# GpSimd's constant loads wait for the low parts of two weight groups in place of the eighth weight piece

## The chip, the cores and the metric

The kernel runs on one core of one Trainium2 chip. The metric is the device time of one execution in microseconds (us), as the median of several runs. A profiled execution gives the rows of the trace; its times count from the start of its span, which is the stretch from its first to its last instruction.

## What is computed

The reference is a stack of transformer blocks over 256 tokens of width 1024, in float32: for each of two layers a gated feed-forward part, a mixer (latent attention in the first layer, attention with forget gates in the second), another feed-forward part and a gated embedding; then a second block with a multiscale pool, dilated attention, gates and a last norm. Only its first step matters here:

```python
h = h + FFN_HALF * swiglu(rms_norm(h, g_ffn1[i]), ffn1_w_in[i], ffn1_w_out[i])

def rms_norm(x, g):
    xf = x.astype(jnp.float32)
    y = xf * lax.rsqrt(jnp.mean(xf * xf, axis=-1, keepdims=True) + EPS)
    return (y * g.astype(jnp.float32)).astype(x.dtype)

def swiglu(x, w_in, w_out):
    gate, up = jnp.split(x @ w_in, 2, axis=-1)
    return (jax.nn.silu(gate) * up) @ w_out
```

The latent attention also needs positions, cosines and sines (`rope`), gains per head and a causal mask. These are the small constants of the change.

## The kernel before

**Weights in groups, each in two parts.** All weights stream from HBM through a ring of four slots. A weight group is 128 x 2048 float32 (1 MB). SyncE fetches it into `raw`; ScalarE rounds it to a high part `wh` (L1538); VectorE subtracts and gives the low part `wl` (L2086) and raises the semaphore `lo_done`; TensorE multiplies three products for each tile, `wh` by the high part of x, `wl` by the high part, `wh` by the low part (L628 to L630). A group of a feed-forward part's input gives 24 matmuls of 512 columns: 4 pieces of 128 rows, 2 tiles of tokens, 3 products. Before a group g TensorE waits for `lo_done` to be g - 1 (`wait_group`, L611), and before a chunk for its PSUM tile to have been read.

**The opening.** Groups 0, 1 and 2 of the first feed-forward part come in twelve pieces of 128 x 512, each with a DMA of its own. The first ten have semaphores of their own, `piece_in[0]` to `piece_in[9]`. ScalarE and VectorE split each piece (L1525, L2074). VectorE's pieces raise `piece_lo`, except for the twelfth, the last of group 2, which raises `lo_done` (DK is 8 here, and k counts from 0):

```python
dve.tensor_tensor(wl[:, k // 4, w], raw[:, k // 4, w], wh[:, k // 4, w].bitcast(F32), ALU.subtract)\
   .then_inc(piece_lo if k < DK + 3 else lo_done, 1)
```

So `lo_done` is 1 when group 2 is done, and 2 when group 3 is.

**The order of the work.** Each engine follows a program written out by hand, in order, and waits on semaphores. Chunk c of the first feed-forward part uses groups 2c and 2c + 1. For chunk 0 ScalarE splits groups up to 3 and then takes the silu of the two token tiles into `sg` (L1633), scaled by `rstd` (it waits for `rstd_done`, in `scaled`), and only then splits group 4. VectorE splits group 3, then multiplies into `a_n` (L2238), waiting for each silu, then splits groups 4 and 5, takes the second pair of `a_n`, and then runs `angles_reduced`, which waits for all eight small loads (`small_in`, L2151) and reads `posi` and `freq` (L2154 on); then groups 6 and 7.

**GpSimd.** Its program is: a memset, the wait of the change (L2942), eight issues of small loads (`tri`, `causal_f`, twice `hraw`, `rgain`, `bf`, `freq`, `posi`; L2943 to L2951), and then `norm(0)`: for each token tile it waits for the sum of squares `ssq` from ScalarE (L1570) and computes `rstd` in two instructions (`inverse_rms`, L2931 and L2932), of which the second raises `rstd_done`.

**SyncE's room.** A fetch of a group g from 6 on waits for `lo_done` to be g - 5 (`room`, L452), so that the slot's old content has been split.

Of the kernel before, what the change touches and what calls it, by code (L numbers as in the profile page):

```python
# [30 lines left out]
DK = D // P  # L31
# [122 lines left out]
def build(nc, I, out):  # L154
    with ExitStack() as ctx:
        def sem(name):
            return ctx.enter_context(nc.semaphore(name))
# [175 lines left out]
        piece_in = [sem(f"piece_in{i}") for i in range(DK + 2)]  # L333
# [4 lines left out]
        lo_done = sem("lo_done")  # L338
# [264 lines left out]
        def _(pe):  # L603
# [201 lines left out]
            def ffn(name, nname, r, after, r_after):  # L805

                g0, q0, _, _ = PLAN[name]

                def chunk(c, i=0):
# [302 lines left out]

            def ple(name, nname, r, after, r_after):
                g, q, _, _ = PLAN[name]
                ready = x_wait(nname)

# [391 lines left out]
        def _(act):  # L1508
# [321 lines left out]
            def ple(name, nname, r, after, r_after):  # L1830

                g, q, _, _ = PLAN[name]

                def sigmoids(t):
                    for n in range(2):
                        tile_ready(act, q + n, t, g + 3)
                        act.activation(gate[:, t, 512 * n:512 * n + 512], acc(q + n, t), ACT.Sigmoid,
                                       scale=scaled(r, t)).then_inc(acc_read[(q + n) % 2], 1)

                norm(nname, r, lambda t: split_to(g + 4), True)  # L1840
                for t in range(NT):
                    squares(r, t)
                sigmoids(0)
                split_to(g + 7)
                sigmoids(1)
                if after != "n8":
                    norm(after, r_after)
                    return

                for n, (t, k) in enumerate(BY_FEATURES):  # L1850
                    round_x(after, r_after, t, k)

                    if n in (8, 9):
                        squares(r_after, n - 8)
# [1065 lines left out]
        def _(pool):  # L2920
            steps = [0]

            def link(ins):

                steps[0] += 1
                ins.then_inc(p_step, 1)
                pool.wait_ge(p_step, steps[0])
# [11 lines left out]
                    link(pool.tensor_scalar(epsn[:, :], ssq[:, :], EPS / D, EPS * EPS, ALU.mult, ALU.add))  # L2939

            link(pool.memset(mhalf[:, :], -0.5))
            pool.wait_ge(piece_in[DK - 1], 16)  # L2942
            pool.dma_start(tri[:, :], I["c_mats"][1]).then_inc(small_in, 16)  # L2943
            pool.dma_start(causal_f[:, :], I["c_mats"][2]).then_inc(small_in, 16)
            for n in range(2):
# [197 lines left out]
```

## Time and profile before

| | us |
|---|---|
| median of 3 runs | 1302.85 |
| lowest, highest | 1302.75, 1304.57 |
| profiled execution, its time | 1302.51 |
| its span | 1300.7 |
| TensorE busy in the span | 1283.2 (99%) |
| VectorE, ScalarE, GpSimd busy | 929.7, 679.3, 125.9 |

The mean granted TensorE clock of the profiled execution is 0.999. A row of a timeline reads: start in us, duration in us, engine, line, operation, output and inputs, count, and in brackets how long the engine had been idle and what released it. Durations overlap a little at their ends, since engines are pipelined; the distance of two starts is the better measure for TensorE. Such a count as x9 merges equal instructions.

### The profile page before, as it was taken

The numbers are of one execution on the slowest core, as the hardware profiler recorded it, in microseconds if no ns is written. First come the engines' busy times: TensorE is split into PE (matmuls) and PEld (weight loads), VectorE is DVE, ScalarE is ACT, GpSimd is POOL, SyncE is SP. The second block draws the span as 40 slices with busy tenths as digits, with TensorE's granted clock in tenths as the row PEclk, the third lists the DMA queues.
The fourth block names the chain that finished last, engine by engine and source line by source line (L and its number), as shares of the span: only waits on it lengthen the run. The fifth ranks groups of instructions, "written<-read, shape, count | busy, mean of one in ns | idle before, by whom it ended". The sixth has DMA issues, their size and how long they took to land.

```text
span 1300.7 us, 16758 instructions
## 1 busy us (share of the span) xinstructions
PE 1283.2 (99%) x6242; PEld 1057.4 (81%) x6242; DVE 929.7 (71%) x1298; ACT 679.3 (52%) x976; POOL 125.9 (10%) x190
## 2 busy tenths in 40 slices
PE   9999999999999999999999999999999999999997
PEld 6888888888888888888887777888888887788886
DVE  6878948986678956677875677667895656655674
ACT  7444537755444546544445567644444735566542
POOL 1000003711000000000001230000000133200000
PEclk9999999999999999999999999999999999999999
DMA  9665645228565655666564643466564496445541
GB/s 311 216 201 189 210 140 203 66 82 263 191 194 194 202 186 162 195 194 194 194 196 158 231 162 119 149 194 194 194 226 154 170 293 215 156 137 179 174 149 33
DMA packets 149505, 236.29 MB, mean 182 GB/s; under 512 B 10080, under 2 KB 104464, under 8 KB 148928
## 3 DMA queue, kind: packets, MB, share of 16 engines
q1 hardware_dynamic: 144432, 222.26, 52.6%
q0 software_dynamic: 4640, 12.81, 3.3%
q8 instruction: 39, 0.64, 0.2%
q10 hardware_dynamic: 368, 0.37, 0.1%
q14 instruction: 26, 0.21, 0.0%
HBM read 233.27 MB, written 4.47 MB: 183 GB/s over the span
## 4 chain that ended last, share of the span: by engine, by line
PE 91%; DVE 4%; ACT 3%; issue 1%; POOL 0%; DMA 0%; POOLq 0%; SPq 0%; ACTq 0%; DVEq 0%
PE acc L628 20%; PE acc L630 20%; PE acc L629 20%; PE acc L661 7%; PE acc L662 7%; PE acc L665 7%; PE misc L704 4%; DVE wl L2086 1%; ACT wh L1538 1%; PE misc L1339 1%; PE misc L888 1%; PE misc L1195 1%; ACT xh L1584 0%; PE acc L868 0%; ACT hn L1570 0%
## 5 line engine op out<-in xcount | busy, mean ns | idle before, releaser
L2086 DVE TENSOR_TENSOR wl<-raw,wh 128x2048 fp32r<-128x2048 f32 x199 | 450.6, 2270 | 183.5 <-ACT wh L1538 182.8
L1538 ACT ACTIVATE wh<-raw 128x2048 fp32r<-128x2048 f32 x205 | 383.5, 1894 | 125.3 <-PE acc L665 104.2
L628 PE MATMUL acc<-wh,xh 128*128 128x512 f32 (+1 forms) x832 | 324.5, 390 | 3.3 <-DVE xl L2132 1.6
L630 PE MATMUL acc<-wh,xl 128*128 128x512 f32 (+1 forms) x832 | 322.5, 388 | 0.0
L629 PE MATMUL acc<-wl,xh 128*128 128x512 f32 (+1 forms) x832 | 322.3, 387 | 0.0
L628 PEld LDWEIGHTS acc<-wh,xh 128*128 128x128 f32 x832 | 156.2, 188 | 36.7 <-DVE wl L2074 1.8
L630 PEld LDWEIGHTS acc<-wh,xl 128*128 128x128 f32 x832 | 156.2, 188 | 32.2
L629 PEld LDWEIGHTS acc<-wl,xh 128*128 128x128 f32 x832 | 156.2, 188 | 31.1
L1633 ACT ACTIVATE sg<-acc,rstd 128x256 f32<-128x256 f32 x88 | 41.4, 475 | 240.4 <-PE acc L630 240.3
L2252 DVE STREAM_TRANSPOSE aT<-a_n 32x384 f32<-32x384 f32 (+1 forms) x256 | 137.1, 536 | 3.9
L661 PE MATMUL acc<-wh,ah 128*128 128x512 f32 x320 | 124.8, 390 | 0.0
L662 PE MATMUL acc<-wl,ah 128*128 128x512 f32 x320 | 124.5, 389 | 0.0
L628 PE MATMUL acc<-wh,zh 128*128 128x512 f32 x272 | 108.6, 399 | 0.5 <-DVE zl L2132 0.5
L630 PE MATMUL acc<-wh,zl 128*128 128x512 f32 x272 | 106.2, 390 | 0.0
L629 PE MATMUL acc<-wl,zh 128*128 128x512 f32 x272 | 106.0, 390 | 0.0
L665 PE MATMUL acc<-wh,al 128*128 128x512 f32 x320 | 98.5, 389 | 0.0
L2931 POOL TENSOR_SCALAR rstd<-ssq 128x1 f32<-128x1 f32 x19 | 9.4, 493 | 886.3 <-ACT hn L1570 886.2
L2238 DVE SCALAR_TENSOR_TENSOR a_n<-acc,rstd,sg 128x256 f32<-128x256 f32 x88 | 42.0, 483 | 48.1 <-ACT sg L1633 48.1
L1584 ACT ACTIVATE xh<-misc,gains 128x128 fp32r<-128x128 f32 x128 | 40.2, 365 | 68.4 <-PE misc L704 60.2
L665 PEld LDWEIGHTS acc<-wh,al 128*128 128x128 f32 x320 | 60.1, 188 | 12.5
L662 PEld LDWEIGHTS acc<-wl,ah 128*128 128x128 f32 x320 | 60.1, 188 | 12.4
L661 PEld LDWEIGHTS acc<-wh,ah 128*128 128x128 f32 x320 | 60.1, 188 | 12.3
(365 smaller groups left out, 1613.1 us busy)
## 6 DMA issues: line engine op xcount, KB each, us to landing
raw<-in_ffn_w_in_dram SPq DMA_DIRECT2D x170, 512.0 KB, 4.8
raw<-in_ffn_w_out_dram SPq DMA_DIRECT2D x88, 512.0 KB, 4.3
raw<-in_w_in_dram SPq DMA_DIRECT2D x64, 512.0 KB, 4.7
raw<-in_fox_w_in_dram SPq DMA_DIRECT2D x24, 512.0 KB, 4.2
raw<-in_ple_w_gate_dram SPq DMA_DIRECT2D x16, 512.0 KB, 4.4
raw<-in_mla_w_o_dram SPq DMA_DIRECT2D x8, 512.0 KB, 4.0
raw<-in_fox_w_o_dram SPq DMA_DIRECT2D x8, 512.0 KB, 4.4
raw<-in_w_out_dram SPq DMA_DIRECT2D x8, 512.0 KB, 4.4
```

Of the source, the lines that this page charges most:

```text
L628: pe.matmul(dst, hi, rhs_h, start=first, stop=False)
L629: pe.matmul(dst, hi, rhs_l, start=False, stop=False)
L630: return pe.matmul(dst, lo, rhs_h, start=False, stop=last)
L661: pe.matmul(acc(q + n, t), xa, wh[:, s, r], start=st, stop=False)
L662: pe.matmul(acc(q + n, t), xa, wl[:, s, r], start=False, stop=False)
L665: mm = pe.matmul(acc(q + n, t), xb, wh[:, s, r], start=False, stop=en)
L704: return pe.transpose(M[0:rows, b, cols], src, m[:, :])
L1538: act.activation(wh[:, s, 0:n], raw[:, s, 0:n], ACT.Copy).then_inc(hi_done, 1)
L1633: act.activation(sg[:, c % 2, t, :], acc(q, t)[:, 0:256], ACT.Silu, scale=rstd[:, t:t + 1]).then_inc(silu_done, 1)
L2086: dve.tensor_tensor(wl[:, s, 0:n], raw[:, s, 0:n], wh[:, s, 0:n].bitcast(F32), ALU.subtract)\
L2238: dve.scalar_tensor_tensor(a_n[:, (c // 3) % 2, t, w], acc(q, t)[:, 256:512], rstd[:, t:t + 1], sg[:, c % 2, t, :], ALU.mult, ALU.mult)\
L2252: e = dve.transpose(dst.rearrange("p c (t i r) -> p t c i r", t=NT, i=4)[:, :, :, i, :], src.rearrange("p t (c o r) -> p t c o r", o=4, r= ...
```

## The change

GpSimd's wait ahead of the eight small loads names another semaphore. Before, it is that of the DMA of the eighth weight piece (the last of group 1). Now it is `lo_done` at 2. Nothing else differs.

```diff
             link(pool.memset(mhalf[:, :], -0.5))
-            pool.wait_ge(piece_in[DK - 1], 16)
+            pool.wait_ge(lo_done, 2)
             pool.dma_start(tri[:, :], I["c_mats"][1]).then_inc(small_in, 16)
             pool.dma_start(causal_f[:, :], I["c_mats"][2]).then_inc(small_in, 16)
```

GpSimd's queue at this place, before; `tri` to `posi` are the small loads, `rstd` the factor of the norm, `piece_in7` the eighth piece's semaphore:

```order
L2943 DMA tri<-in_c_mats_dram 128x128 [waits piece_in7,p_step]
L2944 DMA causal_f<-in_c_mats_dram 128x128
L2946 DMA hraw<-in_head_gains_dram 64x4 x2
L2947 DMA rgain<-in_rope_gains_dram 128x64
L2949 DMA bf<-in_fox_b_f_dram 128x16
L2950 DMA freq<-in_c_freq_dram 128x16
L2951 DMA posi<-in_pos_dram 128x2
L2931 ISA
L2931 TENSOR_SCALAR rstd<-ssq 128x1 [waits sq_done]
L2932 TENSOR_TENSOR rstd<-rstd,mhalf 128x1 [waits p_step]
```

The first of these rows is the only one that differs afterwards; the rows behind it stand in the same order:

```order
-L2943 DMA tri<-in_c_mats_dram 128x128 [waits piece_in7,p_step]
+L2943 DMA tri<-in_c_mats_dram 128x128 [waits lo_done,p_step]
 L2944 DMA causal_f<-in_c_mats_dram 128x128
 L2946 DMA hraw<-in_head_gains_dram 64x4 x2
```

ScalarE's queue is the same before and now. Around the first silu pair (`wh` are high parts, `sg` the silus) it reads:

```order
L1525 ACTIVATE wh<-raw 128x512 [waits raw_in2] x2
L1570 ACTIVATE hn,ssq<-h 128x1024 [waits x_in2,x_in3,x_in1,x_in0] x2
L1538 ACTIVATE wh<-raw 128x2048 [waits raw_in3]
L1633 ACT_TABLE_LOAD [waits rstd_done]
L1633 ACTIVATE sg<-acc,rstd 128x256 [waits acc_ready]
L1633 ACTIVATE sg<-acc,rstd 128x256 [waits rstd_done,w_used]
L1538 ACTIVATE wh<-raw 128x2048 [waits w_used,raw_in0]
```

The wait for `rstd_done` stands at the load of the activation table, ahead of the silu itself, and the high part of group 4 behind both silus. Nothing has moved in it, nor on TensorE, VectorE and SyncE.

## Rows read from the trace of the kernel before

**Rows 1.** The page: span, busy time and instructions, chain by engine and by line.

```profile
span 1300.7 us, 16758 instructions
...
PE 1283.2 (99%) x6242; PEld 1057.4 (81%) x6242; DVE 929.7 (71%) x1298; ACT 679.3 (52%) x976; POOL 125.9 (10%) x190
...
PE 91%; DVE 4%; ACT 3%; issue 1%; POOL 0%; DMA 0%; POOLq 0%; SPq 0%; ACTq 0%; DVEq 0%
```

**Rows 2.** Timeline of ScalarE, 20 to 25 us: start, duration, what, idle before.

```profile
20.91 1.91 ACT L1538 ACTIVATE wh<-raw 128x2048 fp32r<-128x2048 f32 x1
22.84 1.28 ACT L1633 ACT_TABLE_LOAD   x1
24.13 0.84 ACT L1633 ACTIVATE sg<-acc,rstd 128x256 f32<-128x256 f32 x2
24.86 1.92 ACT L1538 ACTIVATE wh<-raw 128x2048 fp32r<-128x2048 f32 x1
```

**Rows 3.** Timeline of VectorE, eighth piece, groups 3 and 4, the positions.

```profile
16.38 0.69 DVE L2074 TENSOR_TENSOR wl<-raw,wh 128x512 fp32r<-128x512 f32 x1 [0.17 <-ACT wh L1525]
...
22.85 2.29 DVE L2086 TENSOR_TENSOR wl<-raw,wh 128x2048 fp32r<-128x2048 f32 x1 [2.86 <-ACT wh L1538]
...
26.82 2.29 DVE L2086 TENSOR_TENSOR wl<-raw,wh 128x2048 fp32r<-128x2048 f32 x1 [0.89 <-ACT wh L1538]
...
32.93 0.11 DVE L2154 CAST posf<-posi 128x2 f32<-128x2 int32 x1
```

**Rows 4.** Timeline of TensorE: end of group 2, start of group 3, start of group 4.

```profile
24.57 0.39 PE L630 MATMUL acc<-wh,xl 128*128 128x512 f32 x1
25.20 0.50 PE L628 MATMUL acc<-wh,xh 128*128 128x512 f32 x1 [0.24 <-DVE wl L2086]
25.53 0.39 PE L629 MATMUL acc<-wl,xh 128*128 128x512 f32 x1
...
30.77 0.39 PE L628 MATMUL acc<-wh,xh 128*128 128x512 f32 x1
```

**Rows 5.** Timeline of GpSimd: first and last of eight issues, first `rstd`.

```profile
14.69 0.76 POOL L2943 DMA_DIRECT2D tri<-in_c_mats_dram  x1 [13.84 <-DMA raw<-in_ffn_w_in_dram]
...
18.68 0.54 POOL L2951 DMA_DIRECT2D posi<-in_pos_dram  x1
20.08 0.18 POOL L2931 TENSOR_SCALAR rstd<-ssq 128x1 f32<-128x1 f32 x1 [0.86 <-ACT hn L1570]
20.34 0.57 POOL L2932 TENSOR_TENSOR rstd<-rstd,mhalf 128x1 f32<-128x1 f32 x1
```

**Rows 6.** Timelines later: VectorE's `wl` and `rstd` beside it, nine issues.

```profile
199.99 2.29 DVE L2086 TENSOR_TENSOR wl<-raw,wh 128x2048 fp32r<-128x2048 f32 x1 [1.43 <-ACT wh L1538]
...
201.08 1.25 POOL L2931 TENSOR_SCALAR rstd<-ssq 128x1 f32<-128x1 f32 x1 [1.84 <-ACT hn L1570]
...
289.04 7.23 POOL L2987 DMA_DIRECT2D bias_repeated<-in_bias_by_offset_dram  x9
```

**Rows 7.** TensorE's last matmul; windows of the tail (columns in the first line).

```profile
1292.58 0.39 PE L630 MATMUL acc<-wh,zl 128*128 128x512 f32 x1
...
core 0: us, PE busy (x) PEld busy (x) DVE busy (x) ACT busy (x) POOL busy (x), PEclk, DMA share, GB/s
...
1297.70:1297.80 0.10, 0.00 (x0) 0.00 (x0) 0.00 (x0) 0.00 (x0) 0.00 (x0) 1.00 0.56 123
1297.80:1297.90 0.10, 0.00 (x0) 0.00 (x0) 0.00 (x0) 0.00 (x0) 0.00 (x0) 0.81 1.93 410
1297.90:1298.00 0.10, 0.00 (x0) 0.00 (x0) 0.00 (x0) 0.00 (x0) 0.00 (x0) 0.50 0.57 123
```

**Rows 8.** Timeline of TensorE: its first nine matmuls, and the last two of them.

```profile
1.25 3.56 PE L608 MATMUL acc<-hn 128*128 128x512 bf16 x9 [1.25 <-DVE hn L2284]
...
4.21 0.60 PE L608 MATMUL acc<-hn 128*128 128x512 bf16 x2
```

**Rows 9.** DMA issues in 0 to 40 us: engine, count, size, us to landing.

```profile
posi<-in_pos_dram POOLq DMA_DIRECT2D x1, 1.0 KB, 6.1
```

## What the change does to the time: the prediction

> **What bounds the kernel now.** I read the page first, then the timelines of the opening 60 us engine by engine, then the waits, then the last 10 us. The page shows TensorE busy for 1283.2 of 1300.7 us, and 91% of the chain that ended last is TensorE [rows 1]. So there is one question for any edit: does it make TensorE wait, or spare it a wait. TensorE cannot work ahead of its weights: each group of 24 matmuls wants both parts of a weight group, `wh` from ScalarE and then `wl` from VectorE. The edit lies in the first 40 us, so the rows to look at are those of groups 3 and 4 there.
>
> Group 3: ScalarE writes its `wh` at 20.91, VectorE its `wl` from 22.85 to 25.14, and TensorE, which had issued its last matmul of group 2 at 24.57, goes on at 25.20 [rows 2 to 4]. TensorE loses 0.24 us there and nothing more until group 4, which it begins at 30.77 without a break [rows 4]. The `wl` of group 4 runs from 26.82 to 29.11 [rows 3], so group 4 is ready 30.77 - 29.11 = 1.66 us before it is wanted. That is the cover of everything ahead of it on ScalarE and VectorE.
>
> What stands ahead of it on ScalarE is the first silu pair. Its table load begins at 22.84, right behind group 3's `wh`; the silus follow at 24.13 and the `wh` of group 4 at 24.86 [rows 2]. The silus scale by `rstd`, and the only writer of `rstd` is GpSimd, which finishes the first value at 20.34 + 0.57 = 20.91 [rows 5], 1.93 us before ScalarE asks. GpSimd issues the eight constant loads just ahead of this: first issue at 14.69, last at 18.68 for 0.54 us [rows 5].
>
> **The change, part by part.**
>
> The wait. The counter `lo_done` is raised neither by group 0 nor by group 1 (their pieces raise `piece_lo`); the first raise comes with the last piece of group 2, the second with the `wl` of group 3. So the value 2 comes at 22.85 + 2.29 = 25.14 [rows 3], not at 14.69. GpSimd has waited 13.8 us there already [rows 5], and will wait 10.5 more. By itself that is free. What is queued behind it isn't: eight issues and then the two `rstd` values, in program order.
>
> The issues. 18.68 + 0.54 - 14.69 = 4.53 us for eight [rows 5]. The same eight instructions move, so I take this value; the nearest other rows are nine issues in 7.23 us, 0.80 each [rows 6], which would make 6.4 us, and the lowest single one is 0.54, which makes 4.3 us. TensorE started 0.06 us after `wl` ended [rows 3, 4]; with the same lag the issues run from 25.20 to 29.73.
>
> The `rstd` values. The sum of squares, which released the first one at 20.08 [rows 5], is there 10 us earlier than it is asked for now, so nothing else is waited for. From the start of the first instruction to the end of the second 20.34 + 0.57 - 20.08 = 0.83 us [rows 5], and 0.10 us for the start: ready at 30.66. Its first instruction took 0.18 us with VectorE idle, but 1.25 us beside a `wl` of VectorE [rows 5, 6]. In the changed kernel VectorE has nothing to do at 29.8, since its next instruction needs the first silu; I take 0.18.
> GPSIMD Engine Reference of the Trainium skill (Specifications) says that GpSimd shares its SBUF interface with VectorE and is held up by VectorE instructions with two SBUF inputs. The two rows agree with that; by it nothing is added here, and if VectorE were busy at that moment the sum would be 1.1 us more.
>
> ScalarE. The order of the program puts the wait for `rstd_done` on the table load, ahead of the silu, so the 1.28 us of the load are not hidden by the wait but come behind it. From the table load's start to the next `wh` is 24.86 - 22.84 = 2.02 us [rows 2]. With 0.04 us of lag: `wh` of group 4 starts at 32.72. The second `rstd` is ready by 31.6, before the second silu asks.
>
> VectorE. From the start of `wh` to the start of `wl` 26.82 - 24.86 = 1.96 us [rows 2, 3], then 2.29 us: 34.68, and done at 36.97. TensorE begins group 4 at 37.03 instead of 30.77: **6.26 us of stall**. Its first matmul after a wait takes 0.33 us to the next one in place of 0.23 [rows 4]: +0.10. Check of the size: `rstd` comes 30.66 - 20.91 = 9.75 us later; of that 1.93 us lay unused before the table load and 1.66 us before group 4, and 0.1 us are the two lags.
>
> The clock. TensorE would sit idle some 6.1 us. In the tail the last matmul is issued at 1292.58 and its record ends 0.39 us later, at 1292.97; the granted clock is still 1.00 up to 1297.8 and falls to 0.50 within the slice that follows, which reads 0.81 [rows 7]: 4.9 us later. An idle time of 6.1 us is longer than that, so I expect the clock to have fallen to 1.2 GHz when TensorE resumes. What this costs, the first matmuls of the run show: of nine the eighth starts at 4.21, seven steps of 0.42 us from 1.25; later they start 0.23 us apart [rows 4, 8]. Seven steps by (0.42 - 0.23) = **+1.4 us**. The bounds are nothing (the clock does not fall) and twice this.
> TensorE: Matmul & The Clock Gate of the Trainium skill (What's actually happening) says that an array which was idle runs at half rate until it has worked for a while. The tail and the opening agree; by it the sum is 1310.3, and without it 1308.9.
>
> What the change takes away. The loads no longer compete with weights between 15 and 25 us. ScalarE has no wait for a weight in that stretch (from 20.91 on its instructions stand back to back) [rows 2], and the 0.24 us of TensorE at 25.20 comes from the length of ScalarE's queue. Worth at most 0.24 us, taken as nothing.
>
> The loads' readers. The slowest landing was 6.1 us after its issue [rows 9]; the last issue at 29.2 gives 35.3. In the kernel before, VectorE reads the positions at 32.93 [rows 3], which would be too early, but in the changed one it first does group 4's and group 5's `wl` (to 39.3) and the second pair of `a_n`, and comes there at about 40. No second wait. Next late would be group 6: angles to 43.2, `wl` to 45.4; TensorE wants it at 37.03 + 2 x 5.45 = 47.9, later still with the slow clock. Cover 2.5 us. SyncE's fetch of group 8 waits for group 4's `wl` as well, 8 us later than before, against a use at 58.8. Behind group 6 every engine waits for TensorE or stands as before relative to it, so nothing makes the loss smaller later on: no wait of this program is for a fixed moment.
>
> **Sum**, against the profiled execution (1302.51 us, 1.81 us around its span, 0.34 us under the median of 1302.85): 6.26 + 0.10 + 1.4 = 7.8 us, 1302.5 + 7.8 = 1310.3 us, +0.6%.
>
> **Rivals.**
> *The clock holds.* The 4.9 us of the tail were one case; if it stays high for over 6.1 us the stall alone is left: 1302.5 + 6.4 = 1308.9.
> *The table load goes ahead of the wait*, as it does at the run's start. Then 1.28 us are hidden: stall about 5.0 us, which is also just short enough for the clock: 1302.5 + 5.1 = 1307.6. The order of instructions speaks against it.
> *The issues are dearer.* At 0.80 us each, as the nine did [rows 6], GpSimd needs 1.9 us more: 1312.2.
> *The issues don't hold GpSimd's arithmetic.* If `rstd` could be computed at once after the wait, the table load starts at 26.2, 3.4 us late, less 1.66: 1302.5 + 1.7 = 1304.2. In the rows before, arithmetic followed the last issue only because its input came later, so they don't exclude it.
> *Not slower: the wait is over sooner than I think.* If the counter's two raises were those of the groups done in pieces (the eighth piece's `wl` ends at 16.38 + 0.69 = 17.07) [rows 3], the issues end at 21.7, `rstd` is ready at 22.6, before 22.84, and nothing moves: 1302.5. It decides at 24.5 = 22.84 + 1.66: whatever has `rstd` ready by then costs TensorE nothing. The code that raises the counter speaks against it.
>
> **How the numbers follow.** Forecast 60%; clock holds 12%; table load ahead 12%; dear issues 8%; issues don't hold 4%; not slower 4% (of which 1% for a gain by less competition of over 0.2%). The forecast's own spread is some 1 us to either side. The range 1307.2 to 1312.3 takes in the first four and leaves out the last two and a little of each edge. A measurement here can tell about 0.2%, 2.6 us: slower 0.92, same 0.07, faster 0.01.
>
> **What would show it.** In the timeline of the changed kernel: GpSimd's first issue at 25.2 and the last ends at 29.7; its first `rstd` at 29.8; ScalarE idle from 22.8 to 30.7 and released by GpSimd; its table load after that and not before; VectorE idle from 25.1 to 32.4; TensorE idle from 30.9 to 37.0, released by `wl` of group 4; a granted clock of under 1.00 near 36 to 40 and some seven matmuls 0.42 us apart; from 45 us on the same rows as before, 7.8 us later. The forecast is wrong if ScalarE's silu does not wait for GpSimd, if TensorE's matmuls after the gap are 0.23 us apart, or if a second wait shows at group 6.

## The result: 1313.23 us, 0.7% slower, and the profile after

| | before | changed |
|---|---|---|
| median, us | 1302.8 (6 runs) | 1313.23 (6 runs) |
| lowest, highest | 1302.62, 1307.5 | 1312.36, 1313.9 |
| profiled execution, its time | 1302.51 | 1313.9 |
| its span | 1300.7 | 1312.1 |

The ratio is 1.0073 (95% interval 1.0063 to 1.0083), +10.4 us. The forecast had the sign and the chain of causes, but not the size: it said +7.8, and the measured median lies 0.9 us above the upper end of its range, 1312.3. The profiled executions stand 11.4 us apart. Four executions of the sets further down, which ran at a mean granted clock of 0.56 to 0.89 and took 1374 to 2172 us, are left out of every median and ratio.

The page of the changed kernel, as [rows 1]: the span, the busy times, and the chain that ended last, by engine.

```profile
span 1312.1 us, 16758 instructions
...
PE 1287.4 (98%) x6242; PEld 1060.5 (81%) x6242; DVE 929.4 (71%) x1298; ACT 678.4 (52%) x976; POOL 125.7 (10%) x190
...
PE 90%; DVE 4%; ACT 3%; issue 2%; POOL 1%; DMA 0%; POOLq 0%; SPq 0%; ACTq 0%; DVEq 0%
```

The instructions are as many as before and no other engine is busier, but TensorE is busy for 1287.4 us in place of 1283.2. So two things came in, read from the sums of busy time alone: time in which TensorE stands (some 7 of the 11.4 us) and time in which it does the same work more slowly (some 4). GpSimd's timeline from 27 us on answers to [rows 5]:

```profile
27.55 0.76 POOL L2943 DMA_DIRECT2D tri<-in_c_mats_dram  x1 [26.70 <-DVE wl L2086]
...
31.53 0.53 POOL L2951 DMA_DIRECT2D posi<-in_pos_dram  x1
32.20 0.18 POOL L2931 TENSOR_SCALAR rstd<-ssq 128x1 f32<-128x1 f32 x1
32.47 0.57 POOL L2932 TENSOR_TENSOR rstd<-rstd,mhalf 128x1 f32<-128x1 f32 x1
```

GpSimd now waits for VectorE's `wl` of group 3, issues eight loads in 31.53 + 0.53 - 27.55 = 4.51 us, and only then computes `rstd`, done at 33.04. ScalarE's timeline shows who asked for it, as [rows 2]:

```profile
22.68 1.92 ACT L1538 ACTIVATE wh<-raw 128x2048 fp32r<-128x2048 f32 x1
33.11 1.28 ACT L1633 ACT_TABLE_LOAD   x1 [8.52 <-POOL rstd L2932]
34.41 0.84 ACT L1633 ACTIVATE sg<-acc,rstd 128x256 f32<-128x256 f32 x2
35.14 1.91 ACT L1538 ACTIVATE wh<-raw 128x2048 fp32r<-128x2048 f32 x1
```

The first line is group 3's high part. ScalarE then stands for 8.52 us where it had stood for none, and the load of the activation table comes behind the wait, not inside it. VectorE, as [rows 3], with the release of GpSimd at the end of its first line (24.63 + 2.29 = 26.92):

```profile
24.63 2.29 DVE L2086 TENSOR_TENSOR wl<-raw,wh 128x2048 fp32r<-128x2048 f32 x1 [2.86 <-ACT wh L1538]
34.92 0.88 DVE L2238 SCALAR_TENSOR_TENSOR a_n<-acc,rstd,sg 128x256 f32<-128x256 f32 x2 [8.00 <-ACT sg L1633]
37.08 4.49 DVE L2086 TENSOR_TENSOR wl<-raw,wh 128x2048 fp32r<-128x2048 f32 x2 [1.28 <-ACT wh L1538]
...
42.42 0.10 DVE L2154 CAST posf<-posi 128x2 f32<-128x2 int32 x1
```

And TensorE, as [rows 4]: the last matmul of group 3, the first two of group 4, then where their distance changes.

```profile
32.32 0.39 PE L630 MATMUL acc<-wh,xl 128*128 128x512 f32 x1
39.51 0.77 PE L628 MATMUL acc<-wh,xh 128*128 128x512 f32 x1 [6.80 <-DVE wl L2086]
40.08 0.63 PE L629 MATMUL acc<-wl,xh 128*128 128x512 f32 x1
...
44.34 0.63 PE L630 MATMUL acc<-wh,xl 128*128 128x512 f32 x1
44.77 0.51 PE L628 MATMUL acc<-wh,xh 128*128 128x512 f32 x1
45.12 0.40 PE L629 MATMUL acc<-wl,xh 128*128 128x512 f32 x1
```

Without a wait group 4 would have begun at 32.32 + 0.23 = 32.55; it begins at 39.51, a **stall of 6.96 us**. Then the starts are 0.43 us apart up to 44.77. The 13 steps from 39.51 to 45.12 take 5.61 us, where 13 of 0.227 us would take 2.95: the **half-rate stretch costs 2.66 us**. The windows of one us around it give the granted clock, the number third from the end of each line:

```profile
34.00:35.00 1.00, 0.00 (x0) 0.00 (x0) 0.08 (x1) 0.99 (x3) 0.00 (x0) 0.89 0.29 4
35.00:36.00 1.00, 0.00 (x0) 0.00 (x0) 0.79 (x2) 1.00 (x2) 0.00 (x0) 0.50 0.01 0
...
44.00:45.00 1.00, 1.00 (x4) 0.81 (x3) 0.86 (x5) 0.00 (x0) 0.00 (x0) 0.50 1.04 340
45.00:46.00 1.00, 1.00 (x5) 0.82 (x5) 0.93 (x4) 0.00 (x0) 0.00 (x0) 0.99 0.99 333
```

The clock is at 1.2 GHz (0.50) while TensorE stands, and stays there for the first 5.5 us of its work, to about 45.

**What remains of the 11.4 us is not from the edit.** This execution lost the clock in the opening too, from 7.6 to 10.8 us, before the two kernels differ at all: GpSimd's first issue of the kernel before is at 14.69 [rows 5]. TensorE's timeline there:

```profile
7.13 0.47 PE L628 MATMUL acc<-wh,xh 128*128 128x512 f32 x1 [1.96 <-DVE xl L2132]
...
8.26 0.63 PE L628 MATMUL acc<-wh,xh 128*128 128x512 f32 x1
8.68 0.63 PE L629 MATMUL acc<-wl,xh 128*128 128x512 f32 x1
...
26.98 0.50 PE L628 MATMUL acc<-wh,xh 128*128 128x512 f32 x1 [0.27 <-DVE wl L2086]
```

Starts 0.43 us apart from 8.26 on, and group 3 begins at 26.98 in place of 25.20 [rows 4]: 1.78 us late. Its first product started 0.29 us later than before (7.13, there 6.84), and the slow stretch makes the other 1.5. The gap ahead of that product is 1.96 us here, the longest of the fourteen profiled executions at this place (1.80 or less in the others, 1.59 in the kernel before), and only here did the clock fall: at about 7.47, 2.3 us after the end of the last matmul ahead of the gap, when TensorE was already at work again. The sum 1.78 + 6.96 + 2.66 = 11.40. A fixed mark later in the program, GpSimd's first `rstd` of the next norm, tests it; these are its rows of the kernel before and of the changed one, with a second mark behind the latent attention:

```profile
198.23 0.38 POOL L2931 TENSOR_SCALAR rstd<-ssq 128x1 f32<-128x1 f32 x1 [176.30 <-ACT hn L1570]
...
305.96 1.25 POOL L2931 TENSOR_SCALAR rstd<-ssq 128x1 f32<-128x1 f32 x1 [9.69 <-ACT hn L1570]
```

```profile
209.68 0.38 POOL L2931 TENSOR_SCALAR rstd<-ssq 128x1 f32<-128x1 f32 x1 [175.73 <-ACT hn L1570]
...
317.42 1.25 POOL L2931 TENSOR_SCALAR rstd<-ssq 128x1 f32<-128x1 f32 x1 [9.71 <-ACT hn L1570]
```

The shift is 11.45 us at the first mark and 11.46 at the second: all of it arises in the first 45 us, and from there to the second mark nothing is given back and nothing is added.

### The profile page after: what moved, and what is told of

It is laid out like the page before. It is cut to its first block, busy times and chain, and to the rows that moved or that the text cites. A ratio compares the mean times of both kernels' runs of the same rounds, so it can differ in the third digit from the quotient of the medians.

```text
span 1312.1 us, 16758 instructions
## 1 busy us (share of the span) xinstructions
PE 1287.4 (98%) x6242; PEld 1060.5 (81%) x6242; DVE 929.4 (71%) x1298; ACT 678.4 (52%) x976; POOL 125.7 (10%) x190
## 4 chain that ended last, share of the span: by engine, by line
PE 90%; DVE 4%; ACT 3%; issue 2%; POOL 1%; DMA 0%; POOLq 0%; SPq 0%; ACTq 0%; DVEq 0%
PE acc L628 20%; PE acc L630 20%; PE acc L629 20%; PE acc L661 7%; PE acc L662 7%; PE acc L665 7%; PE misc L704 4%; DVE wl L2086 1%; ACT wh L1538 1%; PE misc L1339 1%; PE misc L888 1%; PE misc L1195 1%; PE acc L868 0%; ACT xh L1584 0%; ACT hn L1570 0%
## 5 line engine op out<-in xcount | busy, mean ns | idle before, releaser
L662 PEld LDWEIGHTS acc<-wl,ah 128*128 128x128 f32 x320 | 60.1, 188 | 12.4
```

Of the source, the lines that this page charges most:

```text
L662: pe.matmul(acc(q + n, t), xa, wl[:, s, r], start=False, stop=False)
```

## The experiments

Two theories stood after this. **A**: `rstd` is late because it is queued behind the eight issues, ScalarE's queue carries that to group 4, and the idle time costs the clock on top. **B**: the late loads themselves cost time, by their traffic beside the weights or by their readers. Three sets were run, each on another chip and beside its own runs of the kernel before: set 1 median 1303.19 (29 runs), set 2 1304.11 (17), set 3 1304.13 (21). Why these medians differ comes out below. Diffs are against the changed kernel, unless they say otherwise.

| | kernel | median, us | ratio to before (95%) |
|---|---|---|---|
| set 1 | `rstd` first, loads late | 1303.94 | 1.0007 (0.9998 to 1.0015) |
| | release at 1 | 1304.88 | 1.0013 (1.0004 to 1.0021) |
| | wait, `rstd`, loads | 1305.24 | 1.0016 (1.0007 to 1.0025) |
| | gap filled, 28 matmuls | 1311.11 | 1.0062 (1.0047 to 1.0077) |
| set 2 | changed kernel again | 1315.01 | 1.0082 (1.0069 to 1.0095) |
| | table loaded early | 1310.79 | 1.0058 (1.0045 to 1.0071) |
| | four loads, `rstd`, four | 1310.08 | 1.0051 (1.0037 to 1.0065) |
| | opening filled | 1302.9 | 0.9991 (0.9983 to 1.0) |
| set 3 | opening filled, again | 1302.8 | 0.9993 (0.9984 to 1.0002) |
| | `rstd` first, opening filled | 1303.75 | 0.9999 (0.999 to 1.0008) |
| | gap filled, 28, again | 1310.56 | 1.0051 (1.0037 to 1.0064) |
| | gap filled, 14 | 1312.6 | 1.0064 (1.0049 to 1.0079) |

### The loads stay late, `rstd` doesn't

```diff
+            norm(0)
             pool.wait_ge(lo_done, 2)
             pool.dma_start(tri[:, :], I["c_mats"][1]).then_inc(small_in, 16)
...
-            norm(0)
```

> The changed kernel with GpSimd's first two rstd values moved ahead of the wait and of the eight loads; the loads still wait for lo_done at 2. Theory (the loss is rstd standing in GpSimd's queue behind the wait and the issues): ScalarE's first silu is at 24.1 again, no TensorE gap at group 4, the whole loss is gone: 1302.8, the loads' late landing (some 35 us against VectorE's reading at 32.9) hidden by the cover of group 6. Rival (the loads cost by their new place in time, by contention with weight fetches or by landing late): still 1308 or more.

This splits the two theories best: the loads wait for the same event as in the changed kernel (first issue at 25.59), only the order of GpSimd's queue differs. Measured +0.75 us, a ratio of 1.0007: nearly all of the loss is gone, ScalarE's table load stands without a wait at 22.98, and group 4 begins without a break. A holds; B is worth little, 0.75 us by the medians, though the interval reaches up to 2 us. What the late loads do is in these rows: VectorE's first instruction behind its wait for all of them, and TensorE's first matmuls of group 6.

```profile
36.63 0.17 DVE L2152 MEMSET ones<- 128x128 f32 x1 [4.40 <-DMA posi<-in_pos_dram]
```

```profile
42.03 0.50 PE L628 MATMUL acc<-wh,xh 128*128 128x512 f32 x1
42.37 0.40 PE L629 MATMUL acc<-wl,xh 128*128 128x512 f32 x1
```

VectorE waits for 4.40 us, since the last load takes 6.9 us to land here, and group 6 starts 0.46 us behind the matmul before it (41.57) in place of 0.23, and its next one 0.34 later: 0.34 us in these two steps, 0.4 with the next few. The run was expected to show nothing there. So the reader's wait that the prediction ruled out exists, but only where `rstd` is early; in the changed kernel it is hidden behind the greater delay.

### Released one group sooner

```diff
-            pool.wait_ge(lo_done, 2)
+            pool.wait_ge(lo_done, 1)
```

> The changed kernel with the wait for lo_done at 1 (end of group 2, 20.0 us in the kernel before) in place of 2. Theory (eight issues hold rstd for 4.5 us): issues from 20.1 to 20.6 on, rstd at 25.6 to 26.1, table load 2.8 to 3.3 us late, less 1.66 of cover: TensorE stalls 1.1 to 1.6 us, too short for the clock to fall: 1304.0 to 1304.5. Rival (issues do not hold GpSimd's arithmetic): 1302.8. Rival (any new gap costs the clock): 1306.5 or more.

The first issue moves to 21.09. ScalarE's and TensorE's rows:

```profile
26.67 1.28 ACT L1633 ACT_TABLE_LOAD   x1 [3.39 <-POOL rstd L2932]
```

```profile
33.08 0.47 PE L628 MATMUL acc<-wh,xh 128*128 128x512 f32 x1 [1.69 <-DVE wl L2086]
```

ScalarE waits 3.39 us and TensorE loses 1.85 (33.08 in place of 31.23). The median is 1.69 us up. The granted clock stays at 1.00 (2.4 GHz) over this gap and the matmuls behind it are 0.23 us apart: this short stall costs its own length and some 0.1 us for its first matmul, no half-rate stretch.

### The wait, then `rstd`, then the loads

```diff
             pool.wait_ge(lo_done, 2)
+            norm(0)
             pool.dma_start(tri[:, :], I["c_mats"][1]).then_inc(small_in, 16)
...
-            norm(0)
```

> The changed kernel with the order wait, rstd, loads in place of wait, loads, rstd: the wait alone holds rstd, the issues no longer. Theory: rstd at about 26.1 to 26.7 (0.06 or 0.63 us after the low part of group 3 at 25.14, then 0.1 + 0.83), table load 3.3 to 3.9 late, less 1.66: stall 1.7 to 2.3 us, no fall of the clock: 1304.5 to 1305.1. Rival (the wait alone makes most of the loss): 1308 or more.

The wait is the changed kernel's; only the issues are no longer between it and `rstd`. GpSimd's and TensorE's rows:

```profile
25.76 0.19 POOL L2931 TENSOR_SCALAR rstd<-ssq 128x1 f32<-128x1 f32 x1 [24.91 <-DVE wl L2086]
```

```profile
33.08 0.47 PE L628 MATMUL acc<-wh,xh 128*128 128x512 f32 x1 [1.68 <-DVE wl L2086]
```

A stall of 1.85 us (33.08 in place of 31.23) and a median 2.05 us up. Of the changed kernel's stall of 6.96, the wait for VectorE makes 1.85 and the eight issues in front of `rstd`, with their later start, the other 5.1. The arithmetic starts 0.17 us after the `wl` that releases it (25.59); a DMA issue in the same place starts 0.63 us after it (26.92 to 27.55, above).

### Four loads, `rstd`, four loads

```diff
             for n in range(2):
                 pool.dma_start(hraw[HD * n:HD * n + HD, :], I["head_gains"]).then_inc(small_in, 16)
+            norm(0)
             pool.dma_start(rgain[:, :, :], bass.AP(I["rope_gains"].tensor, 0, [[0, P], [ROPE, 2], [1, ROPE]]))\
...
-            norm(0)
```

> The changed kernel with rstd after four of the eight loads (2.37 us of issues) in place of after all eight (4.5 us). Theory (each issue ahead of rstd delays TensorE by its own duration): stall 7.0 - 2.14 = 4.8 us. With a fallen clock 2.5 us more: 7.4 us over the kernel before; with a full clock 4.9 us over it. Rival (the eight issues cost as a whole, by the queue of transfers): as the changed kernel, 10.4 us over.

The middle point between the two, on GpSimd and on TensorE:

```profile
29.12 0.18 POOL L2931 TENSOR_SCALAR rstd<-ssq 128x1 f32<-128x1 f32 x1
```

```profile
36.43 0.76 PE L628 MATMUL acc<-wh,xh 128*128 128x512 f32 x1 [4.66 <-DVE wl L2086]
```

The stall is 4.81 us, and the clock was lost again: from 36.43 to 40.73 ten steps take 4.30 us in place of 2.27, which costs 2.03. By the rows that is 6.8 us; the median is 6.0 us up (7.4 was expected, with 2.5 us for the clock). With the runs above the rows show four times: ScalarE's wait at the table load, less 1.5 to 1.6 us, is TensorE's stall.

| | ScalarE waits | TensorE's stall | difference |
|---|---|---|---|
| release at 1 | 3.39 | 1.85 | 1.54 |
| wait, `rstd`, loads | 3.41 | 1.85 | 1.56 |
| four loads, `rstd`, four | 6.37 | 4.81 | 1.56 |
| changed | 8.52 | 6.96 | 1.56 |

The difference is close to the cover of group 4, 1.66 us in the prediction; the 0.1 us between them is put down to lags.

### The changed kernel once more

No edit; to have it beside the kernels of its set.

> The changed kernel again, beside the others of this set. Theory: stall of 7.0 us at group 4 in every execution, since it is made of fixed durations, and matmuls at half clock behind it, whose number may differ from the twelve of the first look. Time 10.4 us over the kernel before. If the 1.8 us by which the opening was later in the first look belong to the change, the first product starts late or runs at half clock here too; if they are chance, the opening is like that of the kernel before.

TensorE's rows, and the window of 0.1 us in which the clock falls:

```profile
38.43 0.77 PE L628 MATMUL acc<-wh,xh 128*128 128x512 f32 x1 [6.80 <-DVE wl L2086]
...
43.26 0.46 PE L630 MATMUL acc<-wh,xl 128*128 128x512 f32 x1
```

```profile
36.50:36.60 0.10, 0.00 (x0) 0.00 (x0) 0.10 (x1) 0.10 (x1) 0.00 (x0) 0.85 0.00 0
```

The stall is 6.96 us again, to the hundredth, and the issue lag 0.63 again. The opening ran at full clock here. The half-rate stretch cost 2.41 us, a little less than in the other execution, and the clock fell 4.94 us after the last matmul's end (31.63), there 2.07 us (34.78 after 32.71). The first mark is at 208.34: 10.11 us late, of which 6.96 + 2.41 = 9.37 are the edit's and 0.70 an opening that was slower by as much without a fall of the clock (`wl` of group 3 from 23.55, before from 22.85 [rows 3]). Between the marks this execution loses more, GpSimd's rows and a window of TensorE's clock:

```profile
208.34 0.37 POOL L2931 TENSOR_SCALAR rstd<-ssq 128x1 f32<-128x1 f32 x1 [175.47 <-ACT hn L1570]
...
317.55 1.25 POOL L2931 TENSOR_SCALAR rstd<-ssq 128x1 f32<-128x1 f32 x1 [9.71 <-ACT hn L1570]
```

```profile
265.00:270.00 5.00, 5.00 (x25) 4.42 (x26) 4.22 (x14) 4.38 (x12) 0.51 (x1) 0.66 0.00 0
```

The distance of the marks is 109.21 us, and 107.73 in the kernel before: 1.48 us more, with a mean granted clock of 0.66 in five us of latent attention (that is 3.4 us at 0.50), where the kernel before has 1.00. The kernel with `rstd` first shows the same in its profile, 109.19 us, 0.66 from 255 to 260, and so does the half of the filler below, 109.24. In the other eleven profiled executions, the first one of the changed kernel among them, the distance is 107.70 to 107.75. So the edit doesn't need this fall to cost its 9.4 us, and the fall doesn't come with the edit each time. That the edit has no part in it isn't shown: all three kernels that show it have the late loads, and the kernel before was profiled only once.

### TensorE kept at work in the gap

```diff
                 for c in range(1, peel):
+                    if g0 == 0 and c == 2:
+                        for _ in range(28):
+                            pe.matmul(M[:, 0, :], xh[:, 0, 0:P], xh[:, 0:2, :].rearrange("p k n -> p (k n)"),
+                                      start=True, stop=True)
                     chunk(c)
```

> The changed kernel with 28 additional matmuls on TensorE between groups 3 and 4, whose results nobody reads; they take 28 x 0.227 = 6.4 us, less than the 7.0 us in which TensorE waits there. The stall stays, only TensorE's idle time is filled. Theory (about 2.5 us of the loss are twelve matmuls at half clock after the gap): clock 1.00 throughout, 2.5 us less than the changed kernel, about 1310.6. Rival (the clock is worth the predicted 1.4 us, the rest is elsewhere): about 1311.8. Rival (the half clock hides nothing and costs nothing at the end): as the changed kernel, 1313.2.

> The changed kernel with 28 additional matmuls, whose results nobody reads, in its gap, a second time, since the first set had only four undisturbed executions. Theory: 8.1 us over the fastest executions of the kernel before, of which 7.0 are the stall: 1310.7 to 1311.4. Rival (the fall of the clock costs 1.4 us in place of 2.4): 1311.8 to 1312.4.

The stall was to stay and the half-rate stretch to go. TensorE's rows of the second of these runs, the added matmuls and group 4's first:

```profile
31.06 6.51 PE L828 MATMUL misc<-xh 128*128 128x512 f32 x28
38.05 0.47 PE L628 MATMUL acc<-wh,xh 128*128 128x512 f32 x1 [0.48 <-DVE wl L2090]
```

Group 4 begins 7.0 us late as before (31.06 to 38.05), the clock reads 1.00 throughout, and the half-rate stretch is down to 0.08 us. The medians are 7.9 and 6.4 us over those of the kernel before, against 10.4 and 10.9 for the changed kernel. That is the half-rate stretch priced by removal: 2.5 to 4.5 us between medians of different sets, which is too coarse to size it, and 2.3 to 2.6 by the rows (2.41 and 2.66, less 0.08).

### Half of the filler

The same with 14 in place of 28.

> The changed kernel with 14 additional matmuls, whose results nobody reads, right behind group 3, so that TensorE still idles 7.0 - 3.2 = 3.8 us before group 4. If the clock falls here too, some eight to twelve matmuls start 0.43 us apart and the time is that of the changed kernel, 10 us over; if it holds, the time is that of the kernel with 28, 8 us over. The two looks at the changed kernel had it fall 2.2 and 5.1 us after the last matmul, so either can be, in part of the executions.

```profile
31.17 3.33 PE L828 MATMUL misc<-xh 128*128 128x512 f32 x14
38.12 0.77 PE L628 MATMUL acc<-wh,xh 128*128 128x512 f32 x1 [3.62 <-DVE wl L2090]
...
42.95 0.57 PE L630 MATMUL acc<-wh,xl 128*128 128x512 f32 x1
```

The same stall, but TensorE idle for 3.62 us in place of 0.48, and that was enough: the clock fell at 36.48, 1.98 us after the last added matmul, and the stretch costs 2.52 us. The median is 2.0 us above that of the kernel with 28, beside which it ran. So a gap half as long costs as much of the clock as the whole one.

### The table loaded ahead of the wait

```diff
+                    if g0 == 0 and c == 0:
+                        act.activation(rs[:, 0, 1:2], gains[:, 0:1], ACT.Silu)
                     silus(c)
```

> The changed kernel with one additional 128x1 silu on ScalarE ahead of the wait for rstd, which reads a constant; so the activation table is loaded at 22.8 us while ScalarE waits for GpSimd. Theory (the table load's 1.28 us stand behind the wait and in the path): stall 5.7 in place of 7.0 us, 1.3 us less than the changed kernel; the clock still falls, about 9.1 us over the kernel before. Rival (the load was hidden): as the changed kernel. Rival (a gap of 5.7 us keeps the clock): 6.5 us over the kernel before.

ScalarE's rows:

```profile
23.25 1.28 ACT L1648 ACT_TABLE_LOAD   x1
24.55 0.20 ACT L1648 ACTIVATE rs<-gains 128x1 f32<-128x1 f32 x1
31.77 0.47 ACT L1633 ACTIVATE sg<-acc,rstd 128x256 f32<-128x256 f32 x1 [7.02 <-POOL rstd L2934]
32.68 0.47 ACT L1633 ACTIVATE sg<-acc,rstd 128x256 f32<-128x256 f32 x1 [0.44 <-POOL rstd L2934]
```

The load is hidden now, but the stall fell by 0.7 us only, to 6.23, where 1.3 were expected: with the first silu earlier, the second one meets the second `rstd` and waits 0.44 us for it. The table load behind the wait had been the cover of the second `rstd`. The median, 1310.79, is 6.7 us up where 9.1 were expected: the half-rate stretch is shorter here (1.73 us), and the base median of this set is a high one, as the next experiment shows.

### The opening's clock

Against the kernel before, which otherwise stays as it is:

```diff
             turn_quarter(0)
+            for _ in range(4):
+                pe.matmul(acc(1, 1), warm[:, 0:P], warm[:, P:P + 512], start=True, stop=True)
```

> The kernel before with four additional warming matmuls, whose results nobody reads, in TensorE's idle 1.6 us between the first transposes and the first product. Theory (the executions of this kernel that take 1.8 to 4.7 us more than the fastest are those in which the clock falls in the opening): the median is the same, 1303, the slower executions are rarer, and the opening shows a clock of 1.00. Rival (their cause is when the first piece lands): spread as before.

> The kernel before with the four additional warming matmuls in the opening, a second time. The first time all eleven executions lay between 1302.5 and 1303.4, while about half of those of the kernel before lay at 1304 to 1306. Theory (the fall of the clock in the latent attention's stage, worth 1.5 us, depends on what TensorE did in the opening): again no execution over 1304. Rival (chance): about half of them at 1304 to 1306.

The ratios, 0.9991 and 0.9993, are within what can be told from no change. Both profiles have the opening at a clock of 1.00, but so has the profile of the kernel before, so they don't show the theory. What can be told is the spread. The 67 runs of the kernel before in the three sets fall into two humps: 32 lie between 1302.3 and 1303.4, 35 at 1304.0 and above (14 of 29, 10 of 17, 11 of 21). All 22 runs with the filled opening lie under 1304 (1302.52 to 1303.96). The humps' medians, 1302.65 and 1304.5, are 1.85 us apart, about what one such fall of the clock costs (1.48 between the marks, 1.5 in the opening), and all 20 runs with a mean granted clock of 0.997 or less are in the upper hump. The other 15 there read 0.998 or 0.999, like the lower hump, so for them a fall of the clock is a guess. No run of the upper hump was profiled, so the share of each cause in it is open. The medians of the kernel before differ by 0.9 from set to set because a median falls into whichever hump holds more runs.

### Both at once

The diff of the first experiment and this last one together.

> The changed kernel's late loads, but with rstd ahead of them, and the four additional warming matmuls in the opening: the two versions that cost nothing, together. Theory: 1302.5 to 1303.5, level with the kernel before at its fastest and 10 us under the changed kernel. Rival (late loads cost something that the spread of the first try hid): 1304 or more.

VectorE and TensorE at group 6:

```profile
36.83 0.17 DVE L2154 MEMSET ones<- 128x128 f32 x1 [4.56 <-DMA posi<-in_pos_dram]
```

```profile
42.23 0.50 PE L628 MATMUL acc<-wh,xh 128*128 128x512 f32 x1 [0.20 <-DVE wl L2088]
```

1303.75, which is 0.95 us above its neighbour with early loads and between what was expected (up to 1303.5) and the rival's 1304: 0.5 us at group 6 by the rows, the rest not located. 3 of its 11 runs are over 1304, so the added matmuls don't keep every run out of that region once the loads are late. So the late loads bring nothing even when nothing is queued behind them. No kernel here beats the one before by more than can be measured.

## Why the prediction was right in sign and short in size

**What failed, in one place.** Two terms of the sum were sized too small. "The clock" stood at 1.4 us, 1.5 with the 0.10 for the first matmul, and measured 2.66 and 2.41; the stall stood at 6.26 us and measured 6.96 both times, since GpSimd's first issue came 0.63 us after its release and not 0.06. Together that is 7.8 forecast and 9.4 to 9.6 measured, which is still inside the range. What carried the medians out of it, 1 us and more, is not placed (below).

**What held.** The wait moved to the end of group 3's `wl`. It is free by itself and costs by what is queued behind it. Eight issues were forecast at 4.53 us, measured 4.51. `rstd` took 0.84 us with 0.18 for its first instruction: 0.83 and 0.18 had been taken. The table load stands behind the wait. From its start to the next `wh` 35.14 - 33.11 = 2.03 us (2.02), from there to `wl` 1.94 (1.96). The clock was lost, so "the clock holds" is out. "The issues don't hold GpSimd's arithmetic" is out: the run with `rstd` ahead of the issues has it 5 us sooner than the changed kernel. "The issues are dearer" is out at 0.56 each. "Table load ahead" is out by its row, and its gain, taken as 1.28 us hidden, would have been 0.7 (the run with the table early): that rival missed the second `rstd`. "Not slower" is out: the release came from group 3.

**The stall: 6.96 in place of 6.26.** The step that failed here is the lag: I took TensorE's 0.06 us after a `wl` [rows 3, 4] for GpSimd's too. Measured, the first issue comes 0.63 us after the `wl`: +0.57 of the 0.70. The rest are small lags, as far as the rows show; TensorE began 39.51 - 39.37 = 0.14 us after its own `wl`. The lag is 0.63 or 0.64 in all of the other kernels whose first instruction after GpSimd's long wait for 2 is a DMA issue; it was 0.30 where GpSimd had computed `rstd` in between (25.29 to 25.59), and 0.17 where arithmetic came first (25.59 to 25.76). Why is open.

**The half-rate stretch: 2.4 to 2.7 in place of 1.5.** That it would come was right. I read its length from one sample, the seven slow steps of the run's first matmuls [rows 8]; "twice this" was its upper bound, and the range left room for only part of it. The runs give more samples:

| | TensorE idle from | clock falls | later by | TensorE resumes | cost, us |
|---|---|---|---|---|---|
| changed, first profile | 32.71 | 34.78 | 2.07 | 39.51 | 2.66 |
| changed, again | 31.63 | 36.57 | 4.94 | 38.43 | 2.41 |
| table early | 31.35 | 34.11 | 2.76 | 37.42 | 1.73 |
| four, `rstd`, four | 31.78 | 33.76 | 1.98 | 36.43 | 2.03 |
| half of the filler | 34.50 | 36.48 | 1.98 | 38.12 | 2.52 |
| release at 1; wait, `rstd`, loads | 31.40 | not at all | | 33.08 | 0.1 |

Between 8 and 12 matmuls ran at half rate, at 0.20 us lost by each. The opening was a low sample too: in ten of the other thirteen profiled executions its nine matmuls take 4.02 us in place of 3.56, all nine at half rate by the distance of their starts (the granted clock reads 1.00 in that stretch, so the distance is the only sign). And a stage of nine matmuls can't show a stretch of twelve. And the one sample of the fall, 4.9 us in the tail [rows 7], was a high one: I held 6.1 us to be too long by comparing it with that, which came out right, but also a stall of 5.0 us to be "just short enough", which did not. The stall of 4.81 us lost the clock, and so did an idle time of 3.62.
TensorE: Matmul & The Clock Gate of the Trainium skill (What's actually happening) says that the number of slow matmuls at a kernel's start differs from run to run of one kernel, and gives 6, 11 and 14 as examples. The runs here show such a spread behind a gap, 12 and 11 in the changed kernel and 8 to 12 over all five; I had cited the section for the effect and not for its spread.

**The profiled run against the median.** The two terms give 6.96 + 2.4 to 2.7 = 9.4 to 9.6 us for the edit, 1312.0 on top of the profiled 1302.5, which the range held. The medians moved by 10.4 and 10.9. The profiled executions differ from the edit's sum by losses elsewhere: 1.78 us in the opening in one, 1.48 in latent attention and a 0.70 slower opening in the other. The kernel before is slower by this much in about half of its runs, and my profiled execution and the median of the three times were without it. I wrote that the profiled execution stood 0.34 us under the median and left it there, though the highest of the three times, 1304.57, belonged to the second hump. Whether the changed kernel has these falls more often isn't settled: all 11 of its runs lie 0.3 us or more above 1312.0, which speaks for it, but two profiles don't make a share. That leaves 1.0 us of the 10.4 and 1.4 of the 10.9 unplaced. Against the lower hump (1302.65) it is more in the second set: 1315.01 is 12.4 us up, some 3 more than the edit's two terms, of which its profile shows 1.48 and 0.70. Nor is it settled what starts the fall in latent attention, a stage without a long wait.

**The loads' readers.** "No second wait" was right for the changed kernel: VectorE reads the positions at 42.42 without waiting, the last load having landed 4.0 us after its issue. My sum of "35.3" from a landing of 6.1 [rows 9] would have been short elsewhere: with weights streaming beside them the loads took 6.9 and 7.1 us. Where `rstd` is early that used up the cover of group 6, 3.4 us in the kernel before (its `wl` is written from 35.91 to 38.20, TensorE wants it at 41.65). Competition with the weights, taken as nothing, was nothing where TensorE had its only wait: with the loads out of the opening, the 0.24 us at group 3 are 0.25 (25.34) all the same.

## What to carry to other kernels

A wait that is moved costs by what stands behind it in its queue: list everything between it and the next thing that another engine asks for, DMA issues included (0.53 to 0.76 us each here), and subtract the cover once, since from there on the bottleneck loses microsecond for microsecond. Where TensorE is the one that stands, price its clock from more than one row (here gaps of up to 1.8 us cost at most 0.1 us on top, one of 1.96 us cost 1.5, those from 3.6 us on 1.7 to 2.7 us). And before a profile's time serves as the base, look whether the single times fall into humps: half of the runs of the kernel before stood 1.85 us above the other half.

## What the runs showed of the hardware that I had not expected

- GpSimd's first DMA issue after a long wait started 0.63 us after the instruction that released it (0.30 where GpSimd had worked 3.5 us before), its first arithmetic 0.17 us after.
- TensorE's clock fell 1.98, 1.98, 2.07, 2.76 and 4.94 us after the last matmul's end in five gaps (4.9 in the tail), and two gaps of 1.7 us left it alone. In the opening it fell 2.3 us after, behind a gap of 1.96 us that was already over, and cost 1.5 us there. A gap of 3.62 us cost 2.52 us on top of itself, one of 6.80 us 2.41 to 2.66.
- The clock also fell in a stage in which TensorE never stood for long: to a mean of 0.66 over five us of latent attention, at a cost of 1.5 us, in one execution of the changed kernel and not in the other. Four added matmuls in the first 7 us went with times without the second hump, 22 of 22 against 32 of 67; with the late loads beside them it was 8 of 11. Whether they act on the opening alone or on a stage 250 us later as well isn't shown.
- Eight small loads, the same bytes, took 3.9 to 4.0 us to land for the last of them when the weights' stream had paused (changed kernel, 22 GB/s from 32 to 34 us and 2 in the next two), 6.1 to 7.1 us when it ran.
